# A mixer's recurrence run on pairs of tokens, and its steps shared out anew among the attention rounds

## What is computed

```
bu    = (u @ b^T) * b_coef            # complex, 32 groups of 16 channels, 64 states each
state[t] = a_bar * state[t-1] + bu[t] # over the 512 tokens, 2048 complex states
y     = Re(state) @ c_re - Im(state) @ c_im + d * u
out   = gelu(y) * sigmoid(gelu(y) @ w_glu + b_glu)
```

## Time and profile before

| | |
|---|---|
| median of 3 runs | 2065.24 us (2062.25 to 2070.86) |
| profiled execution | 2072.4 us, span 2070.5 us |
| mean granted TensorE clock | 0.963 |
| PE busy | 1975.8 us, 95% of the span |
| DVE, ACT, POOL busy | 1247.4, 846.2, 387.3 us |

### The profile page before, as it was taken

One profiled execution on the slowest core, in us unless ns is written; L12 is line 12 of the kernel. 1 busy time (PEld: TensorE's weight loads), 2 busy tenths in 40 slices (PEclk: granted clock), 3 DMA queues, 4 the chain that ended last, 5 costly groups with the idle time before them and its releaser, 6 DMA issues.

```text
span 2070.5 us, 21878 instructions
## 1 busy us (share of the span) xinstructions
PE 1975.8 (95%) x8614; PEld 1516.5 (73%) x8614; DVE 1247.4 (60%) x1646; ACT 846.2 (41%) x1269; POOL 387.3 (19%) x343
## 2 busy tenths in 40 slices
PE   7999999989977899999999999999999899999997
PEld 5888888766532478888888777776788778766786
DVE  6764344597796445655664776925773468536742
ACT  5331333201445633322333446645552357455531
POOL 2000000156244010100001202512400013214102
PEclk9999999998778899999999989999999999999998
DMA  4232232221000124554552222222122222220221
GB/s 185 85 126 82 95 107 97 85 64 71 26 0 1 66 79 164 196 202 148 198 200 75 82 91 80 82 82 82 52 91 92 97 83 82 91 83 31 92 92 61
DMA packets 53317, 196.69 MB, mean 95 GB/s; under 512 B 5984, under 2 KB 6496, under 8 KB 52704
## 3 DMA queue, kind: packets, MB, share of 16 engines
q1 hardware_dynamic: 43200, 160.55, 22.3%
q0 software_dynamic: 7504, 28.58, 4.1%
q10 hardware_dynamic: 2512, 6.18, 0.9%
HBM read 192.14 MB, written 2.10 MB: 94 GB/s over the span
## 4 chain that ended last, share of the span: by engine, by line
PE 77%; DVE 16%; ACT 4%; issue 2%; POOL 1%; DMA 1%; SPq 0%; POOLq 0%; DVEq 0%; ACTq 0%
PE PS L571 76%; DVE AR L1590 3%; DVE WLO L1587 3%; DVE AR L1823 2%; DVE AR L2072 1%; ACT WHI L1116 1%; PE PS L790 1%; DVE TMP L2146 1%; DVE AR L1913 1%; DVE AR L2039 0%; DVE HNL L1590 0%; DVE ACC L1590 0%; DMA RAW<-in_w13a 0%; DVE H L1975 0%; POOL ACC L2322 0%
## 5 line engine op out<-in xcount | busy, mean ns | idle before, releaser
L1587 DVE TENSOR_TENSOR WLO<-RAW,WHI 128x1024 fp32r<-128x1024 f32 (+1 forms) x272 | 378.3, 1394 | 509.2 <-ACT WHI L1116 509.2
L571 PE MATMUL PS<-HNH,WHI 128*128 128x512 f32 x1632 | 657.9, 403 | 16.0 <-ACT HNH L1147 14.1
L571 PE MATMUL PS<-HNH,WLO 128*128 128x512 f32 x1632 | 640.6, 393 | 3.8 <-DVE WLO L1587 3.8
L1116 ACT ACTIVATE WHI<-RAW 128x1024 fp32r<-128x1024 f32 (+1 forms) x272 | 297.6, 1095 | 648.0 <-PE PS L571 577.1
L571 PE MATMUL PS<-HNL,WHI 128*128 128x512 f32 x1632 | 436.7, 390 | 0.4
L571 PEld LDWEIGHTS PS<-HNH,WHI 128*128 128x128 f32 x1632 | 308.6, 189 | 96.9 <-issue 22.3
L571 PEld LDWEIGHTS PS<-HNH,WLO 128*128 128x128 f32 x1632 | 308.8, 189 | 78.7 <-issue 9.3
L571 PEld LDWEIGHTS PS<-HNL,WHI 128*128 128x128 f32 x1632 | 307.3, 188 | 66.4 <-DVE HNL L1590 2.6
L2202 POOL TENSOR_TENSOR ACC<-ACC,SQ 128x512 f32<-128x512 f32 x46 | 62.9, 1367 | 786.4 <-ACT SQ L1131 785.4
L571 PE MATMUL PS<-AR 128*128 128x512 f32 (+12 forms) x652 | 181.9, 515 | 6.5 <-DVE SQ L1807 5.8
L571 PEld LDWEIGHTS PS<-AR 128*128 128x128 f32 (+5 forms) x652 | 86.3, 203 | 76.8 <-issue 53.0
(11 more groups left out here) (314 smaller groups left out, 2475.6 us busy)
## 6 DMA issues: line engine op xcount, KB each, us to landing
RAW<-in_w_in SPq DMA_DIRECT2D x80, 512.0 KB, 3.5
AR<-in_w_ada POOLq DMA_DIRECT2D x48, 512.0 KB, 3.8
RAW<-in_w13a SPq DMA_DIRECT2D x44, 512.0 KB, 3.2
RAW<-in_w13b SPq DMA_DIRECT2D x44, 512.0 KB, 4.2
RAW<-in_w_out SPq DMA_DIRECT2D x40, 512.0 KB, 3.5
RAW<-in_w2a SPq DMA_DIRECT2D x16, 704.0 KB, 4.1
RAW<-in_w2b SPq DMA_DIRECT2D x16, 704.0 KB, 5.5
RAW<-in_w_inA SPq DMA_DIRECT2D x12, 512.0 KB, 3.3
```

Source lines behind the costliest of these rows:

```text
L571: return pe.matmul(o, l, r, start=start, stop=stop, skip_group_check=True)
L1116: act.activation(hi_of(name, i), raw_of(name, i), ACT.Copy).then_inc(*HI.up(name, i))
L1587: dve.tensor_tensor(lo_of(name, i), raw_of(name, i), f32(hi_of(name, i)), S_).then_inc(*LO.up(name, i))
```

## The change

Two tokens are taken at once: state[t] = a_bar^2 state[t-2] + a_bar bu[t-1] + bu[t] is scanned for every second token only, 256 instead of 512 columns, and the outputs of the tokens between come from the state one pair earlier and a direct term.

- U is stored with the even tokens first, then the odd (`halves`), and read back in order in `s5_out` and `low` (`in_order`, `pairs_of`).
- Drive: four matmuls for each tile, with weights SA (a_bar times B) on even and SB on odd tokens, 256 columns each, both tiles issued together at j = 0, one bank for a tile with the real part in its left and the imaginary part in its right half. DVE then needs two 128x512 operations for a tile, POOL two of 256 columns.
- Scan: pieces c = 0 and 1 alone, one carry; RHO is squared, the tables turn by the double angle.
- Back: DVE 256 columns, POOL one of 256 and one of 512.
- Read: one matmul of 64 rows with THRU (the direct term), then for each of four inputs CpR/CpI for the odd tokens and CaR/CaI (times a_bar) for the even ones, 256 or 255 columns.
- Parameters: CaR, CaI, ATr, ATi on DVE; PE transposes ATr and ATi (8) and forms THRU with 32 matmuls of 32x32 outputs (`s5_weights`) behind tile pair 6 of FFN a; DVE copies the results; the tables are built from step 9 of `side` on, into the first two w2 tiles. POOL loads `s5_bc` in two DMAs, half as much again, and clears RR.
- Order: `some(2)` in the query tiles, `1 if n % 3 == 2 else 2` in the rounds: a block has 8 steps, 64 in all, 26 before the rounds.
- The load of c on POOL waits for the last w_out tile, since OL now lies where CB will.

```diff
-            for c in range(4):
+            for c in range(2):
                 yield "scan", b, c
-        yield from some(3)
+        yield from some(2)
-        yield from some(2)
+        yield from some(1 if n % 3 == 2 else 2)
...
-        OH, OL = tiles_(place("OH", at_ar, 8 * T, F32R)), tiles_(place("OL", at_ar + 9216, 8 * T, F32R))
+        OH, OL = tiles_(place("OH", at_ar, 8 * T, F32R)), tiles_(place("OL", at_ar + 8 * T, 8 * T, F32R))
...
+            def s5_weights():
+
+                for z, src in enumerate((ATr, ATi)):
+                    ps, b = take(pe, "s5_a", z)
+                    pe.wait_ge(*V.at("s5_at"))
+                    for y4 in range(4):
+                        t = pe.transpose(ps[:, P * y4:P * y4 + P], src[:, 4 * y4:4 * y4 + 4, :].rearrange("p a b -> p (a b)"), IDENT)
+                    t.then_inc(*P_.up("s5_a", z))
+                    give(b, V, "s5_a", z)
+                ps, b = take(pe, "s5_thru")
+                for t16 in range(16):
+                    y4, r = t16 // 4, 32 * (t16 % 4)
+                    o = ps[r:r + 32, P * y4 + r:P * y4 + r + 32]
+                    mm(o, BTr[:, t16, :], CpR[:, t16, :], True, False)
+                    t = mm(o, BTi[:, t16, :], CpI[:, t16, :], False, True)
...
-                    mm(psR[:, :], SBr[r, y4, :], U[r, y4, :], True, True).then_inc(*P_.up("drive_re", t16))
-                    mm(psI[:, :], SBi[r, y4, :], U[r, y4, :], True, True).then_inc(*P_.up("drive_im", t16))
+                    if j == 0:
+                        for half, (even, odd) in enumerate(((SAr, SBr), (SAi, SBi))):
+                            for e, w in enumerate((even, odd)):
+                                for x, (ps, _) in enumerate(bs):
+                                    r = slice(32 * (2 * (b % 2) + x), 32 * (2 * (b % 2) + x) + 32)
+                                    ts[x] = mm(ps[:, HT * half:HT * half + HT], w[r, y4, :], U[r, y4, HT * e:HT * e + HT], e == 0, e == 1)
...
+                    mm(ps[r, 0:HT], THRU[r, y4, r], U[r, y4, 0:HT], True, False)
                     for z in range(4):
-                        for j in range(2):
+                        for now in (True, False):
+                            for j in range(2):
...
+                                if now:
+                                    t = mm(o[:, HT:T], w[:, t16, :], x, False, z == 3)
+                                else:
+                                    t = mm(o[:, 1:HT], w[:, t16, :], x[:, 0:HT - 1], False, z == 3)
...
+                ar_, ai_ = bc(are, 2, b3), bc(aim, 2, b3)
+                for o, (x1, y1), (x2, y2), op in ((CaR, (CpR, ar_), (CpI, ai_), A_), (CaI, (CpI, ar_), (CpR, ai_), S_),
+                                                  (ATr, (BTr, ar_), (BTi, ai_), S_), (ATi, (BTi, ar_), (BTr, ai_), A_)):
+                    tt(w1, x1, y1, M_)
+                    tt(w2, x2, y2, M_)
+                    tt(o, w1, w2, op, "s5_at")
...
-                    if half == 0 and i < 10:
+                    if half == 0 and (i < 4 or i in (7, 8) or 9 <= i < 13):
                         next(params, None)
-                        next(params, None)
+                        if i not in (7, 8):
+                            next(params, None)
...
-                    dve.tensor_tensor(f4(vr), f4(psR[:, :]), c4, M_).then_inc(*V.up("drive_a", t16))
-                    dve.tensor_tensor(f4(t1), f4(psI[:, :]), s4, M_).then_inc(*V.up("drive_b", t16))
-                    dve.tensor_tensor(f4(vi), f4(psI[:, :]), c4, M_).then_inc(*V.up("drive_im", t16))
-                    dve.tensor_tensor(f4(t2), f4(psR[:, :]), s4, M_).then_inc(*V.up("drive", t16))
+                    dve.tensor_tensor(f4(V_[b % 2][:, j, :]), f4(ps[:, :]), c4, M_).then_inc(*V.up("drive_a", t16))
+                    dve.tensor_tensor(f4(S5T[j]), f4(ps[:, :]), s4, M_).then_inc(*V.up("drive", t16))
...
-            pool.dma_start(AR[:, 4096:6144], D["s5_bc"]).then_inc(*loaded("s5_bc").up())
+            pool.dma_start(AR[:, 4096:5120], D["s5_bc"][:, 0:1024]).then_inc(*loaded("s5_bc").up())
+            pool.dma_start(AR[:, 0:2048], D["s5_bc"][:, 1024:3072]).then_inc(*loaded("s5_bc").up())
+            pool.memset(RR, 0.0).then_inc(*G.up("s5_zero"))
...
-                    pool.tensor_tensor(f4(S5T[2 * j]), f4(vr), s4, M_).then_inc(*G.up("back_re", t16))
+                    pool.tensor_tensor(f2(S5T[j][:, 0:HT]), f2(v[:, 0:HT]), s2, M_).then_inc(*G.up("back_re", t16))
-                    pool.tensor_tensor(f4(vr), f4(vr), c4, M_).then_inc(*G.up("back_vr", t16))
-                    pool.tensor_tensor(f4(vi), f4(vi), c4, M_).then_inc(*G.up("back_vi", t16))
+                    pool.tensor_tensor(f4(v), f4(v), c4, M_).then_inc(*G.up("back_v", t16))
```

More of the change, by code:

```diff
@@ L458, in program @@
         SBr, SBi = ar(4096, 4, P), ar(4608, 4, P)
-        CR, CI = ar(5120, 16, 32), ar(5632, 16, 32)
+        SAr, SAi = ar(5120, 4, P), ar(5632, 4, P)
         CpR, CpI = ar(6144, 16, 32), ar(6656, 16, 32)
-        U = ar(7168, 4, T)
-        SMALL = AR[:, 9216:9216 + 256]
+        CaR, CaI = ar(7168, 16, 32), ar(7680, 16, 32)
+        CR, CI, BTr, BTi, ATr, ATi = (ar(512 * i, 16, 32) for i in range(6))
+        SW1, SW2 = AR[:, 3072:3584], AR[:, 3584:4096]
+        TW1, TW2 = AR[:, 8448:9472], SQ[:, :, :].rearrange("p a t -> p (a t)")
+        THRU = RR.rearrange("p (y o) -> p y o", o=P)
+        U = ar(8192, 4, T)
+        SMALL = AR[:, 8192:8192 + 256]
+        HT = T // 2
         RHO = AR[:, 20784:20800]
@@ L468, in sm @@
             return SMALL[:, 16 * i:16 * i + 16]
-        V_ = [[ar(at_v, 2, T) for at_v in pair] for pair in ((9216, 10240), (11264, 12288))]
-        XAp = ar(5120, 2, T)
+        V_ = [ar(10240 + 1024 * i, 2, T) for i in range(2)]
+        XAp = ar(12288, 2, T)
         XBp = ar(19456, 16, 2, 31)
-        CEf = ar(5120, 1024)
+        CEf = ar(12288, 1024)
         CE = CEf.rearrange("p (a b c) -> p a b c", b=8, c=32)
@@ L613, in ffn @@
                         give(b1, V, "prod", z, half, mi)
+                        if z == "a" and (half, mi) == (0, 6):
+                            s5_weights()
                     for m in range(KD):
@@ L1614, in s5_params @@
             def s5_params():
-                dt, x, th, k, r, cs, sn, t1, t2, arr, aii, br, bi, den = (sm(i) for i in range(14))
+                dt, x, th, k, r, cs, sn, t1, t2, arr, aii, br, bi, den, are, aim = (sm(i) for i in range(16))
                 lr, li = vec("a_re"), vec("a_im")
@@ L1676, in s5_params @@
                 yield
+                ar_, ai_ = bc(are, 2, b3), bc(aim, 2, b3)
[4 more added lines that the diff above has]
+                    tt(o, w1, w2, op, "s5_at")
+                    if o is CaI:
+                        yield
+                tt(t1, cs, cs, M_)
+                tt(t2, sn, sn, M_)
+                tt(sn, cs, sn, M_)
+                tt(cs, t1, t2, S_)
+                ts(sn, sn, 2.0, None, M_)
+                yield
+                for z, o in enumerate((SAr, SAi)):
+                    dve.wait_ge(*P_.at("s5_a", z))
+                    dve.tensor_copy(o, bank("s5_a", z)[:, :].rearrange("p (y n) -> p y n", n=P)).then_inc(*V.up("s5_a", z))
+                yield
+                dve.wait_ge(*P_.at("s5_thru"))
+                dve.wait_ge(*G.at("s5_zero"))
+                for j in range(4):
+                    r = slice(32 * j, 32 * j + 32)
+                    dve.tensor_copy(THRU[r, :, r], bank("s5_thru")[r, :].rearrange("p (y o) -> p y o", o=P)[:, :, r]).then_inc(*V.up("s5_thru", j))
+                yield
+                dve.wait_ge(*G.at("sq", "n1", 7))
+                mine()
                 dve.tensor_copy(TC[:, :, 0:1], cs.unsqueeze(2)).then_inc(*V.up("s5"))
```

128 lines of the change are left out of this document (71 added, 57 removed).

## The result

The changed kernel takes 2017.63 us in the median of 4 runs (2016.58 to 2018.62), the kernel before 2063.74 in the runs beside it (4, 2061.61 to 2070.86): a ratio of 0.9771, 95% interval 0.9745 to 0.9796, 46 us less. The profiled executions lie further apart, 2070.5 and 2015.2 us of span, since that of before (2072.4 us) was slower than any of the runs above: 55 us is what the two traces have to explain.

What follows compares the result with a forecast made beforehand. VectorE's lateness was taken to hold up TensorE in the mixer. First stretch -17.9, rounds -18.3, costs +6.6 sum to -29.6 us: 2072.4 profiled becomes 2042.8, less 7.2 for the median 2036; range 2006 to 2058 (8 in 10).

Steps and rivals of the forecast that it cites:

- The relief: VectorE's recurrence work in the mixer falls from 141 to 65 us, so 76 us leave.
- D: Rival: a 256-column TensorE instruction costs what a 512-column one does; 28 us slower, 2093; chance 0.05.
- E: Rival: half the width saves only a quarter of TensorE's recurrence time; -5 us, 2060; chance 0.04.
- Idle time: TensorE's idle time falls by 8 us ahead of round 0 and by 12, half of it, in the rounds.
- Both gaps named ahead of round 0: TensorE's waits of 3.8 us at the first squeeze and 3.9 us before the values would go.
- the load that was to be late next there: Ahead of round 0, the load of w_inV would be late next; 1.3 us left idle.
- The half clock: Less TensorE time at 1.2 GHz: -8 us ahead of round 0, -9 in the rounds, a third of at most 29.
- B: Rival: TensorE becomes the only bound; 45 to 67 us faster, 1998 to 2020; chance 0.15.
- A: The forecast itself, with half to one and a half of its sum: -15 to -45 us, 2020 to 2050; chance 0.53.
- Lock-step: Rounds: the reduce-to-scores chain over two rounds, an 8 us lap, becomes the bound; plain rounds 4 us, read rounds 6.
- Rival C: Lock-step or clock takes VectorE's place at once, rounds gaining 0 to 3; +1 to -15 us, 2050 to 2066; chance 0.23.
- Costs: +6.6 us: s5_weights 1.8 plus 3.8, start 1; strided views 0, VectorE's 11 us of side work hidden in the FFN.

Runs made afterwards that it cites:

- e2: Changed kernel plus 112 unread reductions on VectorE behind the recurrence steps, to make it as busy as before: 2065.6 us, ratio 1.0001 to the kernel before.
- e6: Changed kernel plus 32 unread 128 x 512 additions on GpSimd, one behind each drive and back step: 2028.7 us, 11.1 over the changed kernel.
- e8: Changed kernel with the sixteen VectorE operations behind the first FFN's fourth tile pair split, half behind the fifth: 2014.5 us, 3.1 under the changed kernel.
- e4: Changed kernel plus eight unread VectorE reductions ahead of round 2's row maxima, making one stall: 2033.5 us, 15.9 over the changed kernel.
- e10: Changed kernel plus unread VectorE reductions only behind recurrence steps in the rounds (62): 2054.9 us, 37.3 over the changed kernel.
- e5: Kernel before with only the step order changed: two steps behind each query tile, the rest spread over rounds 0 to 22: 2062.7 us, ratio 0.9989.
- e11: Changed kernel plus unread VectorE reductions only behind recurrence steps ahead of round 0 (50): 2027.7 us, 10.1 over the changed kernel.
- e1: Kernel before without the scans of tokens 256 to 511 and their carries, some 39 us less VectorE work: 2049.7 us, ratio 0.9919.
- e7: Changed kernel with the transposes and small matmuls of s5_weights issued twice: 2023.3 us, 5.7 over the changed kernel.
- e9: Changed kernel with the transposes and small matmuls of s5_weights issued four times: 2026.7 us, 9.1 over the changed kernel.

## Why the prediction was right and where it was not

*Direction and mechanism.* Right. VectorE was the late engine, and e2 shows that without its relief there is no gain, to within some 2 us. The size was short: by the traces the change gave 55.3 us where the sum had 29.6. Of the 25.7 missing, the clock is 15, rounds 24 to 31 and the end, for which the sum had no term, 3.2 (the maxima there span 47.2 us in place of 50.0), the costs 3.9 and idle time 3.6.

*The relief.* 76 us were reckoned. The groups sum to 37.8 + 21.8 + 8.1, with carries of 2.6, 70 us in place of 65. The scans are most of the miss: 37.8 us, 0.59 of VectorE's time each, where the sum took 33, because a GpSimd instruction meets no smaller share of them than before: 15 of 64 last over 0.6 us, where 22 of 128 did. VectorE is 75% busy from 415 to 447 (24.0 of 32 us) and not 60%. GpSimd's half-wide instructions take 0.74 and 0.81 us and the wide one 1.34, 58 us with the second drive's 11.9, where 55 stood; its relief has no term of its own in the sum, and e6, which puts back 35 of the 51 us, costs 11.

*TensorE's shapes.* Right: a read takes 4.15 us (4.1 forecast) and a drive pair 1.93 (2.05). Rivals D and E fell with it.

*Idle time.* Nearly right in size. By windows it fell from 35.1 to 11.5 us, 23.6, where 20 was taken. Both gaps named ahead of round 0 are gone, and the load that was to be late next there was not.

*The half clock: the step that failed.* The sum took -8 and -9 for it, "a third, -9, because 528 to 559 was at 0.50 with 29.5 of 31 us busy, which no shorter gap mends". By the windows, the two stretches are 52 us shorter and began 2.7 later, 54.7 in all. Less 23.6 of idle time and plus 0.8 for TensorE's work as forecast, the clock gave about 32 where 17 were in the sum. The half-level time there fell from 95 to 17 us. The step that failed is the inference from row to rule: that the work of 528 to 559 runs at half clock by its nature, so that relief cannot mend it. The changed kernel runs most of that work, and e8 all of it up to 537, at 1.00; e4 brings the half clock back with one stall, e10 with VectorE's load. What started the old spell, behind a wait of 0.33 us, and why the clock stays down so long through this work, stays open. The row "against B" was thus no evidence against B. B's own marks hold ahead of round 0 (clock 1.00, never idle) and not in the rounds (0.93, where it wanted over 0.95, and 11.5 us idle): the truth is A's idle time with nearly B's clock.

*The split.* From the column sums to round 0's first maximum the traces have 134.7 and 106.8 us, from there to round 24's 145.2 and 118.4: 27.9 and 26.8 less, where 17.9 and 18.3 stood. The split of before is the order's doing: e5 alone moves it, to 110.3 and 159.1. By e11 and e10 the relief is worth 10 and 37 us there.

*Lock-step.* The rounds took 118 us (125 forecast), with the rescale as the longest wait, 16.5 us (14). Rival C fell: the rounds take 4.9 us, not 6.

*Costs.* +6.6 were forecast, and the mixer's first matmul, the column sums, came 2.7 us later (391.2 in place of 388.5). s5_weights took 1.75 us and not 5.6: the 64 small instructions took 0.79, 0.012 each, below both bounds of the estimate. At the start nothing was lost: ScalarE's squares wait 3.8 us for GpSimd in place of 2.5, but its tenth weight tile is begun at 59.8 us, and at 60.9 before. The side work on VectorE, costed at nothing under its cover, stopped TensorE once for 1.80 us, because sixteen instructions stood in one piece ahead of a low half of the weights.

*Against the median.* The spans of the two profiled runs differ by 55.3 us and the medians by 46.1, so a sum that was right for the traces would have given 2065.2 - 55.3 = 2009.9, 8 us below the measured median. The sum's shortfall of 25.7 us against the traces shows as only 18 in the median for that reason; this is chance, since the profiled run of before was a slow one of its kernel and that of the changed kernel was not.

## What to carry to other kernels

Where a stretch runs at half clock, do not take it as given by the work that runs in it: look at what stands ahead of it, and whether another version runs the same work at full clock. Where a stall stands ahead, count both as one cost. An engine off the chain is priced by whether its relief takes it below the pace of the loop: half of the relief gave the rounds 3 us (e1), all of it, with the lighter GpSimd, some 41 against e5. To find out which part of a compound change pays, put the old load back on one engine with work that nobody reads: it took one kernel to show that little else counted, and two to show where. Compare the load put back with the load taken off, and compare stretches by the program's own marks, not by fixed times.

## What the hardware showed

- One stall of 6.0 us of TensorE was followed by 22 us of work at 1.2 GHz (e4). In the kernel before, 30.7 us at 1.2 GHz began with no wait over 0.33 us in the 28 us ahead. Gaps of 1.8 us at 84 were followed by 1.00 in one profile and 0.59 in another.
- Half-clock spells are not at the same place in each kernel or execution: rounds 24 to 31 took 47.2 or 50.2 us with the same instructions and nearly the same waits. A cost of 1.5 us was measured as 5.7 (e7), and e9's runs spread over 10.6 us. Effects of some 5 us in a kernel of this kind are not to be read from a median alone.
- The 64 instructions of 32 columns into 32-row outputs began 0.012 us apart in the mean (0.79 us). The Trainium skill (TensorE: Matmul & The Clock Gate, Back-to-back issue gap) gives small matmuls a floor of about 25 ns. The mean lies below it, but the trace does not refute it: the outputs go to four groups of columns of the array, and late in the block the instructions start in fours, within some 3 ns, with about 30 ns to the next four. Four times as many in a row ran into a gap of 2.9 us at which nothing was waited for, while an instruction transfer ran (e9). Its cause was not tried.
- A scan of 128 x 128 takes 0.46 us, and 0.9 to 1.5 where it begins during a GpSimd operation (mean 1.3 in 14 cases).
